# Cross attention turned to channel-major, a head-major forget gate, and merged gate/up matmuls grouped by width

## What is computed

```
def swiglu(h, w_gu, w_down):
    gate, up = jnp.split(h @ w_gu, 2, axis=-1)
    return (jax.nn.silu(gate) * up) @ w_down

log_f = jax.nn.log_sigmoid((zf + b_f[l]).astype(jnp.float32))
c = jnp.cumsum(log_f, axis=1).transpose(0, 2, 1)
s = s + cq_i[..., None] - c[:, :, None, :]

s = jnp.einsum('bshd,bmhd->bhsm', q, k) * (XHEAD_DIM ** -0.5)
p = jax.nn.softmax(s, axis=-1)
o = jnp.einsum('bhsm,bmhd->bshd', p, v).reshape(B, S, D_MODEL)
return o @ w_o
```

## Time and profile before

| | |
|---|---|
| time, median of 3 | 1566.6 us (1564.68 to 1567.84) |
| the profiled execution's own time | 1566.79 us |
| its span, first to last instruction | 1564.5 us |
| busy share of the span: PE, PEld, DVE, ACT, POOL | 99%, 86%, 62%, 48%, 3% |
| mean granted TensorE clock | 0.993 |
| mean DMA rate | 179 GB/s |

### The profile page before, as it was taken

One profiled execution on the slowest core, in us unless ns is written; L12 is line 12 of the kernel. 1 busy time (PEld: TensorE's weight loads), 2 busy tenths in 40 slices (PEclk: granted clock), 3 DMA queues, 4 the chain that ended last, 5 costly groups with the idle time before them and its releaser, 6 DMA issues.

```text
span 1564.5 us, 22731 instructions
## 1 busy us (share of the span) xinstructions
PE 1541.5 (99%) x8810; PEld 1349.5 (86%) x8810; DVE 967.6 (62%) x992; ACT 756.3 (48%) x839; POOL 50.2 (3%) x76
## 2 busy tenths in 40 slices
PE   9999999999999999999999999999999999999997
PEld 8888888888888899989888887888899989888886
DVE  4556766657665745765666666666664666476665
ACT  5544544446444534544544445444445444364444
POOL 0210000000000000000100000000000000000000
PEclk9999999999999999999999999999999999999999
DMA  9544455455555454343455554555544354255552
GB/s 364 191 153 176 159 190 193 180 188 194 196 181 196 148 213 162 135 162 135 162 188 188 188 188 171 203 179 198 192 168 182 120 177 174 97 183 193 181 194 108
DMA packets 39640, 279.57 MB, mean 179 GB/s; under 512 B 4368, under 2 KB 4624, under 8 KB 6160
## 3 DMA queue, kind: packets, MB, share of 16 engines
q1 hardware_dynamic: 38848, 275.27, 48.4%
q10 hardware_dynamic: 720, 3.29, 0.6%
HBM read 277.49 MB, written 1.05 MB: 178 GB/s over the span
## 4 chain that ended last, share of the span: by engine, by line
PE 97%; DVE 1%; issue 1%; DMA 0%; ACT 0%; POOL 0%; POOLq 0%; ACTq 0%; DVEq 0%
PE ps L338 95%; PE ps L523 2%; PE ps L553 0%; DMA res<-x_in 0%; DVE res L1436 0%; DVE Pb L1416 0%; PE ps L532 0%; DVE PTb L1413 0%; PE ps L513 0%; ACT Pb L1226 0%; DVE qk_tok L1775 0%; POOL stat L1805 0%; DVE Vx L1383 0%; DVE xmax L1757 0%; PE ps L850 0%
## 5 line engine op out<-in xcount | busy, mean ns | idle before, releaser
L1257 DVE TENSOR_TENSOR w_lo<-raw,w_hi 128x2048 fp32r<-128x2048 f32 x252 | 576.4, 2291 | 321.1 <-ACT w_hi L889 320.7
L338 PE MATMUL ps<-xT,w_hi 128*128 128x512 f32 (+1 forms) x2984 | 727.7, 345 | 0.0
L889 ACT ACTIVATE w_hi<-raw 128x2048 fp32r<-128x2048 f32 (+1 forms) x255 | 484.6, 1900 | 361.3 <-PE ps L338 347.7
L338 PEld LDWEIGHTS ps<-xT,w_hi 128*128 128x128 f32 x2984 | 478.9, 191 | 20.8
L338 PE MATMUL ps<-xT,w_lo 128*128 128x256 f32 x2304 | 478.5, 281 | 0.0
L338 PEld LDWEIGHTS ps<-xT,w_lo 128*128 128x128 f32 x2304 | 409.0, 190 | 53.8
L338 PE MATMUL ps<-w_hi,sT_hi 128*128 128x512 f32 x576 | 185.8, 391 | 0.8 <-DVE Vx L1383 0.8
L338 PE MATMUL ps<-w_hi,xT 128*128 128x512 f32 (+2 forms) x640 | 186.3, 385 | 0.0
L338 PE MATMUL ps<-w_lo,sT_hi 128*128 128x512 f32 x576 | 184.9, 390 | 0.0
L338 PE MATMUL ps<-w_hi,sT_lo 128*128 128x512 f32 x576 | 184.8, 390 | 0.0
L338 PEld LDWEIGHTS ps<-w_hi,xT 128*128 128x128 f32 x640 | 118.1, 193 | 24.3 <-issue 1.3
(11 more groups left out here) (165 smaller groups left out, 848.3 us busy)
## 6 DMA issues: line engine op xcount, KB each, us to landing
raw<-stream_in SPq DMA_DIRECT2D x256, 1024.0 KB, 4.8
kTx<-mem_in ACTq DMA_DIRECT2D x2, 1024.0 KB, 6.5
res<-x_in SPq DMA_DIRECT2D x2, 512.0 KB, 5.8
kTx<-mem_in SPq DMA_DIRECT2D x1, 1024.0 KB, 9.3
cu<-gate_bias_in SPq DMA_DIRECT2D x1, 1024.0 KB, 14.5
qk_tok<-post_gain_in ACTq DMA_DIRECT2D x1, 1024.0 KB, 5.0
out<-Vx SPq DMA_DIRECT2D x2, 512.0 KB, 3.1
cst<-consts_in SPq DMA_DIRECT2D x1, 512.0 KB, 7.7
```

What stands on the lines that cost most here:

```text
L338: return nc.tensor.matmul(bank_ap, lh, rh, start=start, stop=stop)
L889: nc.scalar.activation(w_hi[:, slot(c), 0:width], raw[:, slot(c), 0:width], copy).then_inc(unit_hi, 1)
L1257: nc.vector.tensor_tensor(w_lo[:, slot(c), :], raw[:, slot(c), :], w_hi[:, slot(c), :].bitcast(F32), sub).then_inc(unit_lo, 1)
```

## The change

Three edits. **In `merged`** all 512-column matmuls of part 0 are issued first, then all 256-column ones; part 1 does the same for each half.

```diff
@@ -472,12 +485,16 @@
                 def tile(f):
                     return slice(f * P, (f + 1) * P)
-                def some(k, fs):
-                    kk = 4 * part + k
-                    for f in fs:
-                        mm(ps[:, b + f, :], wh[:, k, tile(f)], xT[:, kk, :, :].rearrange("p a n -> p (a n)"), kk == 0, False)
-                    for f in fs:
-                        last = mm(ps[:, b + f, 0:S], wl[:, k, tile(f)], xT_hi[:, kk, :], False, kk == KT - 1)
+                def some(ks, fs):
+                    for k in ks:
+                        kk = 4 * part + k
+                        for f in fs:
+                            mm(ps[:, b + f, :], wh[:, k, tile(f)], xT[:, kk, :, :].rearrange("p a n -> p (a n)"), kk == 0,
+                               False)
+                    for k in ks:
+                        kk = 4 * part + k
+                        for f in fs:
+                            last = mm(ps[:, b + f, 0:S], wl[:, k, tile(f)], xT_hi[:, kk, :], False, kk == KT - 1)
                     return last
                 if part == 0:
@@ -492,14 +509,12 @@
                             for f in range(4):
                                 mm(ps[:, b + f, S:2 * S], wh[:, k, tile(f)], xT_lo[:, k, :], False, False)
                         pe.wait_ge(turn_lo, tiles + 2)
-                    for k in range(0 if tiles is None else 2, 4):
-                        last = some(k, range(4))
+                    last = some(range(0 if tiles is None else 2, 4), range(4))
                 else:
                     if tiles is not None:
                         pe.wait_ge(turn_lo, tiles + BT)
                     for fs in ((0, 1), (2, 3)):
-                        for k in range(4):
-                            last = some(k, fs)
+                        last = some(range(4), fs)
                         if fs[0] == 0:
                             last.then_inc(half_sem, 1)
                             if between is not None:
```

```diff
@@ -737,16 +753,10 @@
                 flipped(L3, m0 + 2, 0, B)
                 flipped(L3, m0 + 3, 1, B)
                 pe.wait_ge(unit_lo, upto_unit(L3, m0 + 4))
-                fw = w_hi[:, slot(m0 + 4), 0:F_COLS].rearrange("p (k n) -> p k n", k=KT)
                 for k in range(KT):
-                    for t in range(TOK):
-                        def hi_pass(o=ps[:, 4 + t, 0:2 * HEADS], x_=xT_hi[:, k, t * P:(t + 1) * P]):
-                            return mm(o, x_, fw[:, k, :], k == 0, k == KT - 1)
-                        if k < KT - 1:
-                            hi_pass()
-                        last = mm(ps[:, 4 + t, 0:HEADS], xT_lo[:, k, t * P:(t + 1) * P], fw[:, k, 0:HEADS], False, False)
-                        if k == KT - 1:
-                            last = hi_pass()
+                    fw = w_hi[:, slot(m0 + 4), k * F_STEP:k * F_STEP + P]
+                    mm(ps[:, 4, 0:S], fw, xT_hi[:, k, :], k == 0, False)
+                    last = mm(ps[:, 4, 0:S], fw, xT_lo[:, k, :], False, k == KT - 1)
                 last.then_inc(unit_used, 1)
                 wait_dve("qT")
                 wide(L3, m0 + 5, 0, A)
@@ -754,9 +764,6 @@
                 wait_dve("kT")
                 flipped(L3, m0 + 7, 0, B)
-                wait_dve("logf")
-                mm(ps[:, 6, 0:S], nlf[:, 0, :], upto, True, False)
-                mm(ps[:, 6, P:S], nlf[:, 1, :], upto[:, 0:P], False, True).then_inc(l_pe.sem, l_pe.one("cT"))
                 flipped(L3, m0 + 8, 1, B)
                 wait_dve("cT")
```

ScalarE's two functions and VectorE's steps work on 8 x 256 numbers (slices of `PTb`); VectorE's part:

```diff
@@ -1599,36 +1619,34 @@
                 did(stt(out=qT, in0=two_banks(0), scalar=DH ** -0.5, in1=over(inv_row, 4), op0=mul, op1=mul), "qT")
                 dve.wait_ge(unit_hi, upto_unit(L3, m0 + 4))
-                fw = w_hi[:, slot(m0 + 4), 0:F_COLS].rearrange("p (k n) -> p k n", k=KT)[:, :, HEADS:]
-                fr = raw[:, slot(m0 + 4), 0:F_COLS].rearrange("p (k n) -> p k n", k=KT)[:, :, HEADS:]
-                nc.vector.tensor_tensor(fw, fr, fw.bitcast(F32), sub).then_inc(unit_lo, 1)
+                fc = forget_cols(w_hi, m0 + 4)
+                nc.vector.tensor_tensor(fc[:, :, F_LOW:F_LOW + HEADS], forget_raw(m0 + 4), fc[:, :, 0:HEADS].bitcast(F32),
+                                        sub).then_inc(unit_lo, 1)
+                did(nc.vector.tensor_tensor_reduce(out=bpick[:], in0=ident[:, 0:HEADS], in1=colsL[:, L_BF:L_BF + HEADS],
+                                                   scale=1.0, scalar=0.0, op0=mul, op1=add, accum_out=bcol[:]), "bcol")
                 unit(5)
                 used(L3, m0 + 3)
                 did(nc.vector.tensor_tensor(kT, two_banks(2), over(inv_row, 4), mul), "kT")
                 unit(6)
                 used(L3, m0 + 4)
-                for t in range(TOK):
-                    last = stt(out=lf[:, 4, t, :], in0=ps[:, 4 + t, HEADS:2 * HEADS], scalar=rs(T_MIX, t),
-                               in1=colsL[:, L_BF:L_BF + HEADS], op0=mul, op1=add)
-                did(last, "f_lo")
-                wait_own("f_lo")
-                for t in range(TOK):
-                    last = stt(out=lf[:, 0, t, :], in0=ps[:, 4 + t, 0:HEADS], scalar=rs(T_MIX, t), in1=lf[:, 4, t, :],
-                               op0=mul, op1=add)
-                did(last, "f")
+                lo, hi = slice(F_LOW, F_LOW + HEADS), slice(0, HEADS)
+                did(nc.vector.tensor_tensor(f_lo[hi], ps[lo, 4, 0:S], inv_row[lo, :], mul), "f_lo")
+                did(nc.vector.tensor_tensor(f_hi[hi], ps[hi, 4, 0:S], inv_row[hi, :], mul), "f_hi")
+                wait_own("f_hi")
+                did(stt(out=f_all[hi], in0=f_hi[hi], scalar=bcol[hi], in1=f_lo[hi], op0=add, op1=add), "f")
                 wait_own("f")
-                did(stt(out=lf[:, 1], in0=lf[:, 0], scalar=-1.0, in1=lf[:, 0], op0=mul, op1=mx), "fabs")
+                did(stt(out=f_abs[hi], in0=f_all[hi], scalar=-1.0, in1=f_all[hi], op0=mul, op1=mx), "fabs")
                 unit(7)
                 wait_act("fln")
-                for c in (0, 32):
-                    last = stt(out=nlf[:, :, c:c + HEADS], in0=lf[:, 0], scalar=0.0, in1=lf[:, 3], op0=ALU.min, op1=sub,
-                               reverse1=True)
-                did(last, "logf")
+                did(stt(out=f_neg[hi], in0=f_all[hi], scalar=0.0, in1=f_ln[hi], op0=ALU.min, op1=sub, reverse1=True), "logf")
+                wait_own("logf")
+                did(nc.vector.tensor_tensor_scan(f_cum[hi], ones[hi, 0:1].to_broadcast([HEADS, S]), f_neg[hi], 0.0, mul, add),
+                    "cum")
                 unit(8)
                 unit(9)
                 wait_act("cT_hi")
-                did(nc.vector.tensor_tensor(cT[32:64, :], ps[32:64, 6, 0:S], cT[32:64, :].bitcast(F32), sub), "cT")
```

```diff
@@ -843,34 +852,43 @@
                             last = mm(ps[:, h, t * S:(t + 1) * S], xqT[:, 2 * h + k, t * P:(t + 1) * P],
                                       kTx[:, 2 * h + k, :], k == 0, k == 1)
                     last.then_inc(l_pe.sem, l_pe.one(f"SX{h}"))
-                for h in range(XH):
-                    wait_act(f"xexp{h}")
+                def x_turn(h):
+                    wait_dve(f"xn{h}")
                     for m in range(2):
                         for t in range(TOK):
                             last = nc.tensor.transpose(ps[:, 4 + h, m * S + t * P:m * S + (t + 1) * P],
                                                        Pb[:, h, t * S + m * P:t * S + (m + 1) * P], ident)
                     last.then_inc(l_pe.sem, l_pe.one(f"PX{h}"))
-                for half in range(2):
-                    for e in range(2):
-                        h = 2 * half + e
-                        if h % 2 == 0:
-                            wait_act(f"PX{h}")
-                        else:
-                            wait_dve(f"PX{h}")
-                        for t in range(TOK):
-                            for m in range(2):
-                                last = mm(ps[:, 2 * half + t, e * XDH:(e + 1) * XDH],
-                                          PTb[:, h, m * S + t * P:m * S + (t + 1) * P],
-                                          Vx[:, m, h * XDH:(h + 1) * XDH], m == 0, m == 1)
-                    last.then_inc(l_pe.sem, l_pe.one(f"OX{half}"))
-                def o_wait(k):
-                    if k % 4 == 0:
-                        wait_dve(f"xo{k // 4}")
-                turn(xq_tok, N, wait=o_wait)
+                def x_values(h):
+                    if h < 2:
+                        wait_dve(f"PX{h}")
+                    else:
+                        wait_act(f"PX{h}")
+                    for d in range(2):
+                        for m in range(2):
+                            last = mm(ps[:, h, d * S:(d + 1) * S], Vx[:, m, h * XDH + d * P:h * XDH + (d + 1) * P],
+                                      PTb[:, h, m * S:(m + 1) * S], m == 0, m == 1)
+                    last.then_inc(turn_T, 1)
+                x_scores(0)
+                x_scores(1)
```

(81 more changed lines are left out.)

10 lines of the change are left out of this document (6 added, 4 removed), and 3 rows, old and new, of the table L_DVE.

## The result

The changed kernel takes 1546.6 us (median of 4 executions, 1545.9 to 1547.1) beside 1566.25 us of the kernel before (4, 1564.7 to 1567.8): ratio 0.9873, 95% interval 0.9861 to 0.9885, 19.7 us less. Forecast were 1548.9 us and 17.9 less. The profiled execution's own time is 1547.14 us, its span 1545.3.

The account below looks back on a forecast made before the run. TensorE, holding 97% of the chain that ended last, was taken to bound the kernel. Terms 2.2 + 3.1 + 1.1 + 5.1 + 6.4 = 17.9 off 1566.8 gave 1548.9 us, with 1544.5 to 1555.5 to hold 8 in 10.

Parts of the forecast that it names:

- Grouping: Gate/up units in merged: longer runs of one width save 46 ns in each of 47 pairs, 2.2 us less.
- Rival B: Merged units: the gap depends on column count alone, so reordering is worth nothing; 1551.1 us, chance 0.13.
- Forget gate: Mixer: 16 matmuls of 256 columns replace 32 narrow ones, 1.92 us instead of 3.5; 3.1 us less in all.
- The sum matmuls: Behind the forget gate: two cumulative-sum matmuls move to VectorE, 0.57 us per layer, 1.1 us less in all.
- The cover for VectorE's new steps: Ahead of mixer unit 8: VectorE keeps about 5 us before TensorE needs the unit, so its new steps cost 0.
- Clock: Behind the forget gate: full-width matmuls end the fall to half clock over 3.4 and 6.8 us; 5.1 us less.
- Rival A: Behind the forget gate: the clock still falls, narrow matmuls not being the cause; 1554.0 us, chance 0.12.
- Cross attention: Second set of transposes goes and little waiting stays: 19.17 to 15.97 us, 3.2 less per layer, 6.4 in all.
- The wait of 0.2 us before the first transposes: Cross attention: first transposes can start at 5.4 us, TensorE has scores until 5.2, so it waits 0.2.
- the value passes: Cross attention: 32 value passes on TensorE, priced at 7.01 us of the 15.67 us left per layer.
- Rival C: Cross attention: waits only move, 1.74 us idle comes back, 3.5 us less instead of 6.4; 1551.8 us, chance 0.11.
- rival D: Merged units: long runs of 512 columns never settle; at 242 ns per matmul 1573.7 us, slower, chance 0.03.

Follow-up runs that it names:

- merged_only: The kernel before with only the new order of the gate/up matmuls: 1562.98 us, ratio 0.9981 to the kernel before.
- low_first: The changed kernel with all 256-column matmuls of part 1 in merged put ahead of its 512-column ones: 1544.71 us.
- forget_wide_stream: The kernel before with the forget gate's 32 matmuls streaming 128 columns each instead of 16 or 8: 1560.32 us, ratio 0.9962.
- narrow_later: The changed kernel with 32 useless matmuls of 8 columns ahead of mixer unit 17 in each layer: 1559.67 us.
- wide_later: The changed kernel with 32 useless matmuls of 256 columns ahead of mixer unit 17 in each layer: 1554.72 us.
- cross_only: The kernel before with only the new cross attention: 1557.38 us, ratio 0.9947 to the kernel before.
- dve_extra: The changed kernel with one useless 0.69 us VectorE operation per head behind cross attention's scalings: 1550.11 us.
- after: The changed kernel with all three edits, first runs: 1546.6 us, ratio 0.9873 to the kernel before.
- after_again: The changed kernel, nothing altered, run a second time on one chip with low_first_again: 1547.02 us.
- low_first_again: The low_first kernel run again on one chip beside the changed kernel: 1545.33 us, beside 1547.02.

## Why the prediction was right, and where its terms were off

1. *Grouping, 2.2 us.* Part 0 was to take 5.54 and part 1 5.59; both came exactly so. A block is 47 ns shorter, alone (merged_only) and in the whole change, 2.2 us over 47 pairs of units. Rival B, a gap that depends on the column count alone, is out: by it the block would have kept its length, and low_first takes off the further 40 ns that the entry cost asks for. What the traces don't tell is why an entry costs something.
2. *Forget gate, 3.1 us.* 16 matmuls in 1.92 us, as forecast. The sum matmuls were worth 0.65 us per layer instead of 0.57. The cover for VectorE's new steps was put at 5 us and is 6; the scan, with no row before, was taken at 0.8 and is 0.68.
3. *Clock, 5.1 us.* Right in cause, shown from both sides: wide matmuls in the old place keep the clock (forget_wide_stream), narrow ones in a new place take it down (narrow_later), wide ones there don't (wide_later). Rival A is out. The size holds for the profiled execution: from the start of the forget gate to unit 7, layer 0 went from 16.12 to 12.83 us (564.13 to 580.25, now 562.92 to 575.75), 1.6 of it the gate and 1.7 the clock. It is no constant, as merged_only and cross_only showed: that the 5.1 us of one profile also fit the medians was in part luck.
4. *Cross attention, 6.4 us.* The mechanism was right, and this is the term that was mis-sized: it measured 2 x 3.46 = 6.9. The wait of 0.2 us before the first transposes came as forecast: they were to start at 5.4 us and start at 5.35, 0.17 late. Too high were the 7.01 us for the value passes: in the earlier trace rows they hold a wait of 0.1 us at the first of them, and without it 32 passes take 6.92 (eight in 1.73, 726.86 to 728.59). Nor did the other 0.1 us of waits show. VectorE's chain was summed of whole durations, 0.86 for reciprocal and two scalings; a link adds about 0.75, since the second scaling starts 0.27 us after the first, not 0.35, and the reciprocal starts before the operation ahead has ended. So the last head's scalings ended at 10.75 us instead of 11.3 and their margin is 1.15 us, not 0.6; that changed a margin and no time. Rival C is out as a result and right as a warning: the first head has no margin and the copy of head 1 is 0.16 us ahead of its values; dve_extra turned such a chain into 1.4 us more per layer.
5. *Slower (rival D).* Sixteen 512s in a row hold 227 ns; nothing grew.

The sum was 17.9, the measured gain 19.7, 1.8 more. 0.5 of it is cross attention, 0.15 the sum matmuls and 0.2 TensorE's pause at the turn of the loop (3.24 us, 3.43 before). 0.5 lies in the first 12 us of the kernel, where the input arrives: the first wide matmul starts at 11.5 instead of 12.0 us. That is not the change's: the profiles have this start anywhere from 11.1 to 12.1 us, and merged_only, which changes nothing there, has 11.1. The remaining 0.4 are the 2.3 us around the span before, 1.8 after; what they hold isn't known.

## What to carry to other kernels

Price a matmul by the distance between starts in a long run of its kind, and look separately at what a change of width costs: with few changes the long-run prices simply apply. Matmuls of a few columns cost more than their time: here they take as long as 128-column ones (3.5 us for 32) and can bring the clock down for what follows, so turn them so that the wide side streams. And when normalization moves to the front of a chain, read the margin at each hand-over, not only at the last, and read it from the starts: a short wait behind a matmul can stand in no bracket.

## What was not expected of the hardware

- 32 matmuls of 8 or 16 columns, back to back with no idle time, were followed by 3.4 to 6.8 us at half the clock in six of the eight places where the profiles of before, merged_only, cross_only and narrow_later have them; the same 32 with 128 columns took the same 3.5 us and were not.
- Going from 256 to 512 columns costs about 27 ns, spread over the first five 512s (233, 236, 228, 233, 231 against 227), and going back gains 6 or 7 ns at the first 256 (113 against 120). The blocks of one kernel repeat to within 3 ns (32 in the layers; 16.592 to 16.595 us in merged_only, 16.593 to 16.594 in the changed kernel).
- The stretch at the lower clock where the layer loop turns is 3.4 us long in some executions and 6.8 in others, of the same kernel too (after and after_again, low_first and low_first_again). TensorE has stood still for 3.2 to 4.5 us there, waiting for nothing that the profiles show.
